# Expert weights by a scatter into DRAM instead of one-hot products on TensorE

## The reference, cut to what matters

```python
q = (xc @ wq).reshape(C, 8, 2, half)
s = einsum('thpd,hpkd->thpk', q, subkeys)       # 8 heads, 2 sides, 128 keys
sv, si = top_k(s, 16)
cand = sv[:, :, 0, :, None] + sv[:, :, 1, None, :]   # 16 x 16 pairs
cid  = si[:, :, 0, :, None] * 128 + si[:, :, 1, None, :]
fs, fi = top_k(cand.reshape(...), 16)
eid = take_along_axis(cid, fi); g = softmax(fs)
a = gelu(einsum('tc,thkc->thk', xc, u_tab[eid]))
out = einsum('thk,thkc->tc', g * a, v_tab[eid])
```

## Time and profile before

| | |
|---|---|
| time before, median of 3 runs | 2020.98 us (2019.01 to 2022.08) |
| span of the profiled execution | 2017.2 us (its own time is not given apart from the span) |
| TensorE busy | 2008.9 us, 100% |
| GpSimd busy | 1603.3 us, 79% |
| VectorE busy | 1298.3 us, 64% |
| ScalarE busy | 1118.2 us, 55% |
| granted TensorE clock | 1.000 of 2.4 GHz over the span |

### The profile page before, as it was taken

The page is one execution under the profiler, slowest core; times in us unless marked ns, Lnnn a source line. Parts: engine busy times, 40 slices in busy tenths (PEclk is TensorE's granted clock), DMA queues, the critical chain, the costliest instruction groups (busy, mean ns, idle before and its releaser), DMA issues.

```text
span 2017.2 us, 42413 instructions
## 1 busy us (share of the span) xinstructions
PE 2008.9 (100%) x12436; PEld 1745.7 (87%) x12436; DVE 1298.3 (64%) x2815; ACT 1118.2 (55%) x2453; POOL 1603.3 (79%) x1316
## 2 busy tenths in 40 slices
PE   9999999999999999999999999999999999999999
PEld 8989888888888888888888898888888888888887
DVE  6787599888887333333378865998888873333333
ACT  6565666654444555555565556556544455555554
POOL 7777879987777888888877677998877778888886
PEclk9999999999999999999999999999999999999999
DMA  9444645544444555555584455555544445555554
GB/s 278 166 145 147 209 162 190 187 169 148 154 146 147 196 190 195 194 191 194 191 244 151 135 178 177 178 185 180 167 155 147 153 149 197 189 196 190 195 193 150
DMA packets 103396, 358.41 MB, mean 178 GB/s; under 512 B 11744, under 2 KB 16802, under 8 KB 103076
## 3 DMA queue, kind: packets, MB, share of 16 engines
q1 hardware_dynamic: 102900, 355.41, 53.0%
q10 hardware_dynamic: 432, 2.18, 0.3%
HBM read 356.49 MB, written 1.05 MB: 177 GB/s over the span
## 4 chain that ended last, share of the span: by engine, by line
PE 71%; POOL 15%; issue 11%; POOLq 0%; ACT 0%; DMA 0%; SPq 0%; DVE 0%; DVEq 0%; ACTq 0%
PE bank L1975 34%; PE bank L1621 21%; POOL w_lo L438 15%; PE bank L1623 10%; PE bank L1914 4%; PE bank L1594 0%; PE bank L1598 0%; PE bank L1596 0%; PE bank L1893 0%; DMA ring<-stream 0%; POOLq L436 0%; POOLq L459 0%; ACT w_hi L501 0%; SPq L403 0%; PE bank L2001 0%
## 5 line engine op out<-in xcount | busy, mean ns | idle before, releaser
L438 POOL TENSOR_TENSOR w_lo<-ring,w_hi 128x512 fp32r<-128x512 f32 x1048 | 1401.4, 1353 | 323.6 <-ACT w_hi L501 322.7
L501 ACT ACTIVATE w_hi<-ring 128x512 fp32r<-128x512 f32 x1312 | 752.5, 620 | 185.4 <-PE bank L1598 131.6
L1621 PE MATMUL bank<-act_parts,w_hi 128*128 128x512 f32 x2048 | 722.8, 398 | 0.4 <-POOL w_lo L438 0.2
L1623 PE MATMUL bank<-act_parts,w_lo 128*128 128x256 f32 x2048 | 569.8, 278 | 0.0
L438 DVE TENSOR_TENSOR w_lo<-ring,w_hi 128x512 fp32r<-128x512 f32 x256 | 236.7, 925 | 450.0 <-ACT w_hi L501 449.8
L1621 PEld LDWEIGHTS bank<-act_parts,w_hi 128*128 128x128 f32 x2048 | 384.2, 188 | 88.9 <-POOL w_lo L438 0.9
L1975 PE MATMUL bank<-w_hi,e_hi 128*128 128x512 f32 x1024 | 398.9, 390 | 0.2
L1975 PE MATMUL bank<-w_hi,e_lo 128*128 128x512 f32 x1024 | 398.4, 389 | 0.0
L1975 PE MATMUL bank<-w_lo,e_hi 128*128 128x512 f32 x1024 | 398.4, 389 | 0.0
L1623 PEld LDWEIGHTS bank<-act_parts,w_lo 128*128 128x128 f32 x2048 | 385.4, 188 | 0.0
L837 ACT ACTIVATE e_hi<-arena 128x256 fp32r (+1 forms) x256 | 106.8, 418 | 316.0 <-PE bank L1975 316.0
(11 more groups left out here) (245 smaller groups left out, 2533.2 us busy)
## 6 DMA issues: line engine op xcount, KB each, us to landing
ring<-stream SPq DMA_DIRECT2D x654, 512.0 KB, 3.3
arena<-rpb_in SPq DMA_DIRECT2D x8, 512.0 KB, 7.3
arena<-dft_in SPq DMA_DIRECT2D x4, 512.0 KB, 5.0
arena<-subkeys ACTq DMA_DIRECT2D x2, 1024.0 KB, 5.7
ring<-stream SPq DMA_DIRECT2D x4, 256.0 KB, 5.4
xT<-x_in SPq DMA_DIRECT2D x4, 256.0 KB, 5.6
arena<-w_in SPq DMA_DIRECT2D x2, 512.0 KB
arena<-decay_in SPq DMA_DIRECT2D x2, 512.0 KB
```

Source lines behind the costliest of these rows:

```text
L438: eng.tensor_tensor(w_lo[:, part_, :], ring[:, tile % RING, half * HT:(half + 1) * HT], w_hi[:, part_, :].bitcast(F32), ALU.subtract).then ...
L501: nc.scalar.activation(w_hi[:, 2 * (tile % AHEAD) + half, :], ring[:, tile % RING, half * HT:(half + 1) * HT], ACT.Copy).then_inc(hi_ready ...
L1621: T.matmul(out_[:, 0:2 * S], weights(w_hi, tile, k), both[:, :, k, :], start=(k == 0), stop=False, skip_group_check=True)
L1623: ins = T.matmul(out_[:, 0:S], weights(w_lo, tile, k), both[:, 0, k, :], start=False, stop=(k == KT - 1), skip_group_check=True)
```

## The change

1. u tiles are computed by `contract` into 256 columns of a bank, all 128 alike; the copying out and adding of a second half is gone, and the gelu reads the bank. `wide_tile` stays for the query tiles.
2. The one-hot rows, their products, the turning of the slots, the ones in `experts` and the multiplications at lines 1515 and 1528 are gone.
3. The sort runs in eight chunks of two heads x one token half. A chunk ends in places (expert number x 256 + token) and weights. Weights of a same expert in earlier heads are added to a later head's by comparing it with all earlier slots of the token (`same_key_sum`), so that the last one written holds the sum. Each chunk has an exp of its own, with table loads around it.
4. A table of 16384 x 256 float32 (16.8 MB) a layer lies in DRAM. SyncE zeroes it by 64 writes of 256 KB behind the loads of stream tiles 20 to 83. GpSimd scatters the weights: 256 indirect DMAs a layer, each of 128 elements of 4 bytes; a head waits until all earlier heads of its token half have landed.
5. After all scatters landed SyncE fetches the table, 128 KB for each v tile, into `g_ring` (four slots), and VectorE multiplies it into the experts of that tile (`weight_experts`) just ahead of their use; ScalarE's `expert_high` waits for that.
6. Low halves: of the u tiles GpSimd makes 0 to 11, 72 to 75 and 100 to 103, VectorE all others, placed among the sort's operations by a running clock; of the v tiles VectorE makes both halves.

The core of the diff, in this order: constants, SyncE, GpSimd, ScalarE over the u tiles, VectorE, TensorE. In `same_key_sum` two more operations of the same shape follow (a product, a sum). The diff also notes a cost for every sort operation as the argument of `worked`: 668, 348 and 672 ns for one score row, 550 for the candidates of a chunk, 611, 319 and 614 for the best of a head, 1300 for the ranks, 1350 for each side's keys, 300, 350 and 150 for places and weights.

```diff
-POOL_TILES = T_VT
+POOL_TILES = T_U + POOL_FIRST        # POOL_FIRST = 12
+POOL_AGAIN = ((72, 76), (100, 104))
+CHUNKS = 8
+EXP_AT = (2, 8, 17, 32, 47, 64, 77, 97)
+TILE_NS, HIGH_NS, HALF_NS, SORT_SHARE = 2880, 650, 740, 1.05
...
+                with sp.Fori(l * GROUPS + ZERO_TURN, l * GROUPS + ZERO_TURN + ZERO_TURNS) as turn:
                     for slot in range(RING):
                         refill(turn, slot)
+                        sp.dma_start(blocks[bass.ds(block_, 1), :, :].rearrange("a p w -> (a p) w"), zero_rows[:, :]
...
+                for slot in range(RING):
+                    refill(first_v, slot)
+                for tt in range(TT):
+                    sp.wait_ge(spread_out[l * TT + tt], 16 * PH * TOPK)
+                for j in range(RING):
+                    load_gates(j, j)
+                with sp.Fori(first_v + 1, (l + 1) * GROUPS) as turn:
+                    for slot in range(RING):
+                        refill(turn, slot)
+                        j = turn * RING + (slot - first_v * RING)
+                        sp.wait_ge(e_made.sem, turn * RING + (slot - first_v * RING + e_made.at(l, 1 - RING)))
+                        load_gates(j, slot)
...
+                def spread_head(c, n):
+                    tt, h = c % TT, 2 * (c // TT) + n
+                    landed = spread_out[l * TT + tt]
+                    pool.wait_ge(slots_made.sem, slots_made.at(l, c + 1))
+                    if h:
+                        pool.wait_ge(landed, 16 * TOPK * h)
+                    for slot in range(n * TOPK, (n + 1) * TOPK):
+                        pool.indirect_dma_start(
+                            gates_of[l], bass.IndirectOffsetOnAxis(ap=place_u[:, c, slot:slot + 1], axis=0),
+                            weight_f[:, c, slot:slot + 1], None).then_inc(landed, 16)
...
+                pool.wait_ge(zero_in.sem, zero_in.at(l, zero_in.per_layer))
+                for c in (0, 2):
+                    for n in range(2):
+                        spread_head(c, n)
+                        spread_head(c + 1, n)
+                spread_head(4, 0)
+                lows_again(*POOL_AGAIN[0])
+                spread_head(5, 0)
+                spread_head(4, 1)
+                spread_head(5, 1)
+                spread_head(6, 0)
+                lows_again(*POOL_AGAIN[1])
+                spread_head(6, 1)
+                spread_head(7, 0)
+                spread_head(7, 1)
...
+                for n in range(NK):
                     high_parts(l, 0, T_U + n + AHEAD)
+                    held.append(n)
+                    if n + 1 in EXP_AT:
+                        load_table(ACT.Exp)
+                    elif n in EXP_AT:
+                        chunk_exp(EXP_AT.index(n))
+                    else:
+                        if n - 1 in EXP_AT:
+                            load_table(ACT.Gelu_apprx_tanh)
+                        for tile in held:
+                            gelu(tile)
+                        held = []
...
+                def worked(ns):
+                    clock[0] += SORT_SHARE * ns
+                    while halves[0] < 2 * NK and clock[0] >= (halves[0] // 2 - 1) * TILE_NS + HIGH_NS * (
+                            1 + halves[0] % 2):
+                        next_low()
...
+                def same_key_sum(tt, n, h):
+                    earlier, count_ = slice(0, h * TOPK), TOPK if h <= 4 else TOPK // 2
+                    for k in range(0, TOPK, count_):
+                        shape = [P, count_, h * TOPK]
+                        own = slice(n * TOPK + k, n * TOPK + k + count_)
+                        same = pairs[:, 0:count_ * h * TOPK].rearrange("p (k s) -> p k s", k=count_)
+                        link(V.tensor_tensor(same, own_ids[:, own].unsqueeze(2).to_broadcast(shape),
+                                             ids_ps[:, tt, earlier].unsqueeze(1).to_broadcast(shape), ALU.is_equal))
+                        worked(80 + 1.05 * count_ * h * TOPK)
...
+                def weight_experts(i, j):
+                    slot = g_in[j % RING]
+                    dve.wait_ge(slot.sem, slot.at(l, i * 16 + 16 * (j // RING + 1)))
+                    w = experts[:, bass.ds(i * RING + j, 1), :].rearrange("p a t -> p (a t)")
+                    V.tensor_tensor(w, w, g_ring[:, j % RING, :], ALU.mult).then_inc(e_made.sem, 1)
...
+                dve.wait_ge(gelu_done.sem, gelu_done.at(l, 3))
+                weight_experts(0, 0)
+                weight_experts(0, 1)
+                low_parts(V, l, 0, T_VT)
+                low_parts(V, l, 0, T_VT + 1)
+                weight_experts(0, 2)
+                dve.wait_ge(gelu_done.sem, gelu_done.at(l, NK))
                 with dve.Fori(0, NK // RING - 1) as i:
                     for s in range(RING):
-                        low_parts(V, l, i, T_VT + s + AHEAD, [0])
+                        low_parts(V, l, i, T_VT + s + AHEAD)
+                        weight_experts(i, s + 3)
...
-                    wide_tile(bank[s % 4], i, T_U + first + s, both_acts)
+                    contract(bank[s % 4][:, 0:S], i, T_U + first + s).then_inc(tile_done.sem, 1)
```

552 lines of the change are left out of this document (209 added, 343 removed).

## The result

The changed kernel takes **2133.82 us** (median of 4 runs, 2132.63 to 2136.77) against 2020.06 before on the same chip: 1.057 times as long, 95% interval 1.0557 to 1.0584. The forecast was 2006 and a faster kernel; the time is outside its range (1968 to 2056). On another chip the same kernel took 2610 us, while the kernel before stayed at 2019; that is a second effect and has a part of its own (the last experiments).

A forecast was written before the change was run, and what follows sets the result against it. TensorE, with work 100% of the span, was taken to bound the kernel. -72.7 + 3 + 4.4 + 51 - 1.6 = -15.9 took the span from 2017.2 to 2001; adding 3.8 and rounding up gave 2006 us, range 1968 to 2056.

The forecast's parts named there:

- the price of a scatter: GpSimd, u stage: each of 256 scatters a layer taken at 0.9 us, between 0.47 and 1.30; hidden up to 1.10.
- Rival 3: U stage: scatters issued too slowly, GpSimd the bound from 1.10 us each; 2025 at 1.20, 2052 at 1.30; chance 0.20.
- TensorE's u stage, 367.1: U stage: 128 tiles at 2.868 us instead of 403.4 us, 36.3 saved a layer, -72.7 us in both.
- VectorE's list: U stage: sort and low halves on VectorE keep TensorE's pace, 5 to 10% ahead of the listed costs; costed at nothing.
- Rival 4: U stage: scatters hold the port, each of 172 VectorE low halves waits 0.45 us; 62 a layer, 2130; chance 0.08.
- ScalarE's exps, +3: U stage: gelus held back around each exp make TensorE 0.2 us late, 16 times, +3 us.
- The border, +4.4: Between u and v stages: table fetch and weighting start v tile 0 some 2.2 us late, +4.4 us.
- The v loop: V stage: closed chain over ScalarE and VectorE takes 2.92 us a tile (2.86 to 2.97) against TensorE's 2.72, +51 us.
- The sum: Whole kernel: -72.7 + 3 + 4.4 + 51 - 1.6 = -15.9, span from 2017.2 to 2001, time 2006 us.
- Zeroes and fetches at nothing: SyncE and DMA engines: 16.8 MB each of table zeroes and fetches fit beside the stream loads, costing nothing.

The follow-up runs named there:

- the last experiments: On a chip of the other kind: the changed kernel, unaltered, 2609.93 us; three edits with GpSimd's first low halves cut from 12 tiles to 8, 2504.11 us.
- three edits: Changed kernel with weighting first in the v loop, no GpSimd low halves after its scatters begin, longer times in VectorE's list: 2034.29 us (1.0073).

## Why the prediction was wrong

**The first step that failed is the price of a scatter**, "I take 0.9, the middle of the bounds: hidden". The mean distance is 1.38 us, above the limit of 1.10 that the same step had worked out, and above its upper bound of 1.30. Rival 3 is what happened, in its places (tile 72, tile 100), with its sign. By its own working at 1.38 the low half of tile 72 is 144 x (1.38 - 1.23) = 21 us late (1.23 is the limit that its 3.3 tiles at 1.30 stand for) and that of tile 100 64 x (1.38 - 1.10) = 18; measured are 12.4 behind 9.5 of gaps near the start, and 16.8. So with the right price the prediction's own sum is about 2006 + 78 = 2084, and not yet 2134. (Its 9.5 us at a price of 1.20 is a slip: 64 x 0.10 is 6.4.) Its size was limited by 1.30, the longest GpSimd operation in the rows. What was missing is that issue time of 0.30 stands between two scatters, long or short, and that VectorE adds 0.35 to one of three. An operation that no row shows was bounded by operations of another kind; the middle of such bounds, 0.9, was the value that decided, and the limit of 1.10 lay between them.

**TensorE's u stage, 367.1**: right as the pace of TensorE. 128 x 2.88 is 368.6, and with all longer stalls removed (three edits) it ran from 255.5 to 629.3, 374, exps and all. It was no longer what sets the end.

**VectorE's list, "I cost this at nothing", is the second step that failed.** With one scatter a head left the u stages are 394 and 391 us for a forecast of 370.8. Of these 23 us in the first layer 12.6 are the three gaps behind VectorE, and some 6 are the slow clock after them. That run's span of 2056.6 is 55 above the 2001 of the sum: 44 in the u stages, some 13 in the v stages, with small changes elsewhere. So the forecast would have missed its range, if barely, with hardly a scatter in the queue. The prices noted in the list had been compared with the rows on one sort operation, the score row, and that held. The chunk's second part costs more. From the timeline of the first chunk:

```profile
262.68 1.32 DVE L1433 CAST norm_tmp<-norm_tmp 128x64 f32<-128x64 uint32 x1
...
266.89 1.25 DVE L1443 CAST index_b<-norm_tmp 128x64 bf16<-128x64 uint32 x1
...
268.17 0.69 DVE L1449 TENSOR_TENSOR q_lo<-rank_b,iota_k 128x512 bf16<-128x512 bf16 x1
...
289.59 0.18 DVE L1433 CAST norm_tmp<-norm_tmp 128x64 f32<-128x64 uint32 x1
```

The same cast takes 1.32 us beside GpSimd's low halves and 0.18 in the second chunk, when GpSimd is waiting; the picks' first operation takes 0.69 in every chunk where 0.45 is noted. From ranks to weights the first chunk took 16.6 us for the listed 5.9. The earlier trace rows had this mark (1406 ns against 428 for one cast), and the prediction used it in the v stage only. The runs show that taking away the gaps near the start won nothing while GpSimd's queue was the bound, and that with few scatters they are what is left.

**Rival 4**, the port lock on VectorE's low halves in the u stage, didn't happen: they have a mean of 0.69 us from 300 to 680 us. It is the other way round: the scatter gets longer, not the low half. Some small operations of VectorE do get longer beside a scatter: the cast above takes 0.41 to 0.42 where it starts during one (320.46, 407.59, 569.34).

The Trainium skill (SBUF — State Buffer, Who interferes with whom) says that a VectorE operation with two SBUF inputs shuts out a GpSimd one that reads SBUF, and infers that such an operation doesn't disturb the emission of a GpSimd DMA. The first part agrees with the v loop, where the pair of low halves that starts during e_lo takes 1.51 us (800.45) and the pair of the u stage 1.29 (400.06). The cast has one input and is no test of it. The second doesn't hold for these scatters, which take 1.31 instead of 0.96 us beside a subtraction of two SBUF inputs, and 0.96 when that is narrow. They also read their places and weights from SBUF; whether that read is what gets longer no run tells.

**ScalarE's exps, +3**: right in kind, too small by half. With three edits all eight of the first layer show, each a distance of 0.57 us between two matmuls that are else 0.12 to 0.19 apart, some 0.4 to 0.5 each, 3 to 4 us a layer for the 1.5 of the forecast. **The border, +4.4**: 2.3 to 2.5 a layer where the scatters are out of the way, as forecast; behind 256 scatters 7.7 and 8.9.

**The slow clock** was in no step. After the stall at tile 72 the granted clock is low for some us; the window that follows it:

```profile
493.70:500.00 6.30, 6.27 (x31) 6.28 (x32) 0.00 (x0) 0.69 (x2) 3.66 (x3) 0.54 0.44 159
```

At a granted clock of 0.54, mostly the 1.2 GHz level, the matmuls of 256 columns come 0.213 us apart and not 0.12. By the length of these low stretches a stall of TensorE of 12 us cost 15, one of 17 cost 19.

**The v loop**: right, 2.94 against the 2.92 taken and inside 2.86 to 2.97; the stages are 31 and 33 us longer and 25 were forecast.

**The sum.** Forecast for the two layers: u stages of 370.8, v stages of 373. Measured: 429.0 and 428.8, 378 and 381. Of the 130 us between 2001 and 2131, 116 are the u stage. Taking nearly all scatters away gives back 35 to 38 us a layer of its 58; the 20 to 23 that then remain lay under GpSimd's queue, which set the whole.

**Zeroes and fetches at nothing**: the stretch under the zero writes kept its length, and the fetches never came last after the border; on the quiet chips this was right.

## What to carry to other kernels

When work is moved to an engine that has no row for it, work out first the price at which it stops hiding; if that lies between your bounds, the forecast is the bound's and not the middle's. A long run of issues on an in-order queue sets the stage as a whole: take first issue, count times distance, and what must follow the last one, and check that against the stage before looking at single stalls. Here the stalls upstream were part of that sum, and removing one moved much or all of the wait elsewhere. When the queue is relieved the next bound is what feeds it: here VectorE's list, whose last chunk comes too late for its own scatters. And the order of two operations in a loop that is closed over three engines was worth 29 us a layer. Whether one scatter with several offsets a partition would cost less for each weight was not run.

## What the runs showed that was not expected

- An indirect DMA of 128 elements on GpSimd: 0.96 us, 0.30 us of issue ahead of each, 1.27 from start to start; 1.61 in 84 of 250 distances, nearly all with a subtraction of 128x512 with both inputs in SBUF on VectorE at the scatter's start; 1.26 in 237 of 248 when that is 64 columns wide.
- On two of the four chips of the experiments, runs of such scatters stop the stream: 15 GB/s for 171, matmuls one at a time, 2610 us for 2132. The kernel without scatters has 2017 to 2021 on all of them. Of the versions with all 256 scatters here, a time from one chip says little about the next.
- A cast of 128x64 from SBUF to SBUF on VectorE: 0.18 us alone, 0.41 to 0.42 where it starts during a scatter, 1.32 beside GpSimd's low halves.
